# The last four gate pairs of the second block as seven products of half the columns

## The chip, the cores and the metric

One core of a Trainium2 chip runs the whole program in one launch. The metric is the device time of that launch in microseconds. Lower is better. Three runs of the kernel before were timed; one further number is that of the profiled execution.

## The reference, cut to what matters

A first transformer block (differential attention, multiscale pooling, MLP) feeds a second one. The sequence has 512 tokens, the model 1024 features, all in float32. The change is in the second block's mixer and in what follows it directly:

```python
proj = h @ w_in[l]
q_a, k_a, v_a, u_b, gate_b, gate_c, g_a, g_b = jnp.split(proj, split_points, axis=-1)
...
branch_a = o_a @ w_branch_a[l]
branch_b = y_b @ w_branch_b[l]
merged = jax.nn.sigmoid(g_a) * branch_a + jax.nn.sigmoid(g_b) * branch_b
x = x + merged @ w_mix_out[l]
x = x + memory_cross_attention(rms_norm(x, norm_mem_q[l]), rms_norm(mem, norm_mem_kv[l]),
                               w_mem_q[l], w_mem_kv[l], w_mem_o[l])
```

`g_a` and `g_b` have 1024 features each, `branch_a` and `branch_b` come from 512 features, and `mem` has 256 rows of 1024 features.

## The kernel before

Activations lie with features on the 128 partitions and the 512 tokens along the free axis, so a matrix product is made in output tiles of 128 features x 512 tokens. A *unit* is the weights of one such tile: 128 output features, 1024 (or 512) input features, held as 128 x 1024 (or 512) numbers. Every value that goes into a product is split into a rounded high part and a remainder, and each 128 x 128 block of weights takes three products: high with high, high with remainder, remainder with high. A 1024-wide unit has 8 blocks and so 24 products of 512 columns, a 512-wide one 12.

The work is written out by hand as one list of steps (`Order.build`), which every engine walks through in order, taking the steps that concern it. `tick` moves a clock on by one half-unit of products; `later(n, step)` puts a step into the list n ticks after the next one, ahead of that tick's products; `drain` ticks until nothing is left waiting. SyncE issues the loads of weights into `RAW` (three places of 128 x 1024), ScalarE rounds them into `WH` or `WTh` (`split`, `split_hi`), VectorE writes the remainder into `WL` or `WTl` (the same step, `split_lo`), TensorE multiplies. `WH` and `WL` have six halves, numbered 4 to 9; `WTh` and `WTl` have four, 0 to 3. `Places` gives each unit its slot: a wide unit gets the next two of the six, in turn, by the count `wide`:

```python
keys = (4 + 2 * (wide % NW), 5 + 2 * (wide % NW))
wide += 1
...
self.free_after.append(max(self.last_in_slot.get(k, -1) for k in keys))
```

ScalarE waits, before it rounds a unit, until the unit that was last in its slot has been multiplied (`free_after`). Outside the stretches with seven products, a unit is rounded `ahead` = 3 units in advance (`split_to`).

Products of units go to the two banks of `G` in turn; a bank is free again when the step that empties it is done (`g_bank`). In `block_b`, for each n of 0 to 7 there are four units: `sa n` and `sb n` (the two gates, 1024 wide), `bb n` and `ba n` (the two branches, 512 wide). The gate's sum is emptied by ScalarE's sigmoid (`gate_b`) into `sgb`; VectorE multiplies the branch's sum into it (`branch`), and `merge_b` adds the two, rounds on ScalarE, and writes the remainder on VectorE. The merged tile n is chunk n of the products `mx 0` to `mx 7` that follow in `memory`, each with its residual addition on VectorE, a scaled rounded copy and a square on ScalarE. GpSimd sums the squares. Beside gates 2 to 6 the memory tokens are loaded, squared, summed, normed by one product (`norm`, `mem`) and split; `km` needs them after `mx`.

Seven products (Winograd's form of Strassen's scheme) are in the kernel in two other places: 12 pairs of up-projection units in the first block (`seven_up`) and 20 pairs in the last feed-forward layer. A pair of units times 512 tokens is seen as a 2 x 2 matrix of blocks times a 2 x 2 matrix, and computed by seven products of 4 blocks x 3 x 256 columns. It needs sums of weight blocks (`tile_sum`, VectorE), sums of activation blocks (`h`, `s13`, `s2`, `s4`, `s_hi`, `s_lo`) and recombination (`one_out` and `c11` on ScalarE, `w_less`, `v_less`, `c22`, `c12`, `c21` on VectorE).

Of the kernel before, what the change touches and what calls it, by code (L numbers as in the profile page):

```python
# [104 lines left out]
MID, MID_FIRST, MID_PAIRS = 100, 4, 12  # L105
AHEAD_M = 6
RAW_MLP = {("up", 0): (0, 1, 2, 0, 1, 2, 0, 1), ("dn", 0): (2, 0, 1, 2, 0, 2, 0, 1), ("dn", 8): PLACES, ("dn", 16): (0, 3, 0, 0, 2, 1, 0, 2),
# [14 lines left out]
def plan():  # L122
# [23 lines left out]
    for n in range(2, 8):  # L146
        u += [("sa", n, 1024), ("sb", n, 1024), ("bb", n, 512), ("ba", n, 512)]
# [32 lines left out]
class Places:  # L180
# [3 lines left out]
    def __init__(self, units):  # L184
        self.slot, self.free_after, self.third, self.nth, self.loads = [], [], [], [], []
        self.pair_nth, self.last_in_slot, self.last_in_third, self.count = {}, {}, {}, [0] * (NRAW + 1)
        wide, half, cycle, raw = 0, 0, (), 0
        third_of = {(name, i + n): t for (name, i), row in RAW_MLP.items() for n, t in enumerate(row)}
        self.plain_held, self.pair_held = [0] * (NRAW + 1), [0, 0]
        for v, (name, i, width) in enumerate(units):  # L190
            if name == "su":
# [29 lines left out]
    def pairs_over(self, third):  # L221

        return max(self.pair_held) if third == 2 else self.pair_held[third % NRAW]
# [14 lines left out]
class Order:  # L238
# [3 lines left out]
    def __init__(self):  # L242
# [8 lines left out]
        self.fetches, self.pairs = self.tail_loads(), [f for f in range(22) if ("st", f, 0) in self.item_of]  # L251
        self.middle = [MID + p for p in range(MID_FIRST, MID_FIRST + MID_PAIRS)]
# [126 lines left out]
    def split_to(self, u, ahead):  # L379
# [6 lines left out]
        halves = sum(width // S for _, _, width in self.units[u + 1:self.split])  # L386
        while self.split < len(self.units):
# [353 lines left out]

    def attention_b(self, start):
# [11 lines left out]
    def block_b(self):  # L754
# [211 lines left out]
def program(nc, a, out):  # L966
# [4 lines left out]
    first_pairs = (order.middle[0:2], order.pairs[0:2])  # L971
    pairs = order.middle + order.pairs
    unit_at = {u: n for n, u in enumerate((name, i) for name, i, _ in units)}
    ctx = ExitStack()
    with ctx:
# [59 lines left out]
        sgb = [(F[:, 2, :], T[:, 7, :]), (F[:, 0, :], F[:, 1, :])]  # L1035
# [103 lines left out]
        SUMS = T[:, S_AT:S_AT + 2, :].rearrange("p a (b s) -> p (a b) s", b=2)  # L1139

        def halves_of(kt):

            return (F[:, 0, :], F[:, 1, :]) if kt % 2 == 0 else (F[:, 2, :], MSK[:, :])
# [8 lines left out]
        def raw_tile(third):  # L1152

            return RAW[:, third, :] if third < NRAW else T[:, 4:6, :].rearrange("p a s -> p (a s)")

        def b_tiles(f):

            return {"t1": T[:, 4 + 2 * (f % 2), :], "t3": T[:, 5 + 2 * (f % 2), :], "b11": RAW[:, f % 2, 0:S],
                    "b21": RAW[:, f % 2, S:2 * S], "b22": RAW[:, 2, f % 2 * S:f % 2 * S + S], "t2": T_SUM[0], "t4": T_SUM[1]}

# [135 lines left out]
        LOADED, LOADED_BEFORE = (*d_raw, d_x[6]), (0, 0, 0, 2)  # L1296
# [6 lines left out]
        SEVEN_ACT, SEVEN_DVE = tally("one_out", "c11", "silu"), tally("w_less", "v_less", "c22", "c12", "c21")  # L1303
# [22 lines left out]
        def pair_source(f):  # L1326

            return (a["up"][2 * (f - MID)], a["up"][2 * (f - MID) + 1]) if f >= MID else (a["fg"][f], a["fu"][f])
# [25 lines left out]
        def _(e):  # L1354
            cst = a["cst"]
            for step in steps:
# [5 lines left out]
                elif kind == "load" and places.loads[arg[0]][0] != "unit":  # L1362
# [5 lines left out]
                    elif name == "sums" and f == MID + MID_FIRST + 1:  # L1368
                        e.wait_ge(prep_dve, PREP_DVE["s_lo", 0, 3])
                    if behind:  # L1370
# [8 lines left out]
                elif kind == "load" and arg[0] > 0:  # L1379
# [8 lines left out]
                    if behind:  # L1388
                        e.wait_ge(w_hi, behind)
                        e.wait_ge(w_lo, behind)  # L1390
                    e.dma_start(raw_tile(third)[:, 0:c], src).then_inc(LOADED[third], 16)
# [2058 lines left out]
```

## Time and profile before

| what | us |
|---|---|
| median of three runs | 1547.46 |
| lowest and highest | 1547.44, 1548.38 |
| profiled execution, its time | 1548.38 |
| profiled execution, its span (first to last instruction) | 1546.6 |
| TensorE busy | 1536.8 |
| VectorE busy | 1055.0 |
| ScalarE busy | 754.5 |
| GpSimd busy | 69.1 |

The span is what the views of the profile divide up; what the time has beyond it lies outside the instructions. A product's record overlaps the next one's, so its cost is read from the distance of two starts, not from its duration. The gates of n = 2 start at 888.08 us, the mix product at 986.48 us.

### The profile page before, as it was taken

The numbers are of one execution on the slowest core, as the hardware profiler recorded it, in microseconds if no ns is written. First come the engines' busy times: TensorE is split into PE (matmuls) and PEld (weight loads), VectorE is DVE, ScalarE is ACT, GpSimd is POOL, SyncE is SP. The second block draws the span as 40 slices with busy tenths as digits, with TensorE's granted clock in tenths as the row PEclk, the third lists the DMA queues.
The fourth block names the chain that finished last, engine by engine and source line by source line (L and its number), as shares of the span: only waits on it lengthen the run. The fifth ranks groups of instructions, "written<-read, shape, count | busy, mean of one in ns | idle before, by whom it ended". The sixth has DMA issues, their size and how long they took to land.

```text
span 1546.6 us, 22323 instructions
## 1 busy us (share of the span) xinstructions
PE 1536.8 (99%) x8348; PEld 1330.0 (86%) x8348; DVE 1055.0 (68%) x1755; ACT 754.5 (49%) x1307; POOL 69.1 (4%) x60
## 2 busy tenths in 40 slices
PE   9999999999999999999999999999999999999998
PEld 7888888888899899888888888888888899989987
DVE  6776887768789575447777545555555899948735
ACT  5446677744457445444544334344444445524514
POOL 0000000020000000210000010020002000000002
PEclk9999999999999999999999999999999999999999
DMA  5333222332323233324351242334123333322322
GB/s 195 122 109 97 88 78 93 103 129 90 127 84 110 96 96 108 97 82 131 118 141 62 71 137 87 118 118 156 55 82 109 110 103 110 124 96 82 110 89 75
DMA packets 56235, 161.88 MB, mean 105 GB/s; under 512 B 7232, under 2 KB 8640, under 8 KB 56000
## 3 DMA queue, kind: packets, MB, share of 16 engines
q1 hardware_dynamic: 55504, 159.41, 31.7%
q8 instruction: 67, 1.10, 0.3%
q0 software_dynamic: 320, 0.52, 0.2%
q10 hardware_dynamic: 304, 0.52, 0.1%
q14 instruction: 40, 0.33, 0.1%
HBM read 148.89 MB, written 2.10 MB: 98 GB/s over the span
## 4 chain that ended last, share of the span: by engine, by line
PE 96%; DVE 2%; ACT 1%; issue 1%; DMA 1%; SPq 0%; DVEq 0%; ACTq 0%
PE G L1490 66%; PE TP L1490 10%; PE SC L1490 9%; PE O L1490 5%; PE M L1490 5%; PE TP L1946 1%; PE TP L1892 0%; DMA T<-QK 0%; DVE WL L2623 0%; DMA GN<-in_gains 0%; PE TP L1995 0%; ACT L2030 0%; SPq L1465 0%; ACT WH L2033 0%; DVE T L2917 0%
## 5 line engine op out<-in xcount | busy, mean ns | idle before, releaser
L1490 PE MATMUL G<-XGh,WH 128*128 128x512 f32 x920 | 362.2, 394 | 0.0
L2623 DVE TENSOR_TENSOR WL<-RAW,WH 128x1024 fp32r<-128x1024 f32 (+2 forms) x269 | 282.7, 1055 | 116.5 <-ACT WH L2033 116.2
L1490 PE MATMUL G<-XGh,WL 128*128 128x512 f32 x920 | 358.4, 390 | 0.0
L1490 PE MATMUL G<-XGl,WH 128*128 128x512 f32 x920 | 358.3, 389 | 0.0
L2033 ACT ACTIVATE WH<-RAW 128x1024 fp32r<-128x1024 f32 (+2 forms) x275 | 240.0, 881 | 93.3 <-PE G L1490 60.8
L1490 PEld LDWEIGHTS G<-XGh,WL 128*128 128x128 f32 x920 | 172.7, 188 | 36.5
L1490 PEld LDWEIGHTS G<-XGh,WH 128*128 128x128 f32 x920 | 172.8, 188 | 36.1
L1490 PEld LDWEIGHTS G<-XGl,WH 128*128 128x128 f32 x920 | 172.9, 188 | 34.3 <-DVE XGl L2623 0.2
L1490 PE MATMUL G<-MGh,WH 128*128 128x512 f32 x372 | 145.0, 390 | 0.0
L1490 PE MATMUL G<-MGl,WH 128*128 128x512 f32 x372 | 144.8, 389 | 0.0
L1490 PE MATMUL G<-MGh,WL 128*128 128x512 f32 x372 | 144.7, 389 | 0.0
L2973 DVE TENSOR_TENSOR X<-X,G 128x512 f32<-128x512 f32 x67 | 46.0, 686 | 132.8 <-PE G L1490 132.7
L1490 PEld LDWEIGHTS G<-MGh,WL 128*128 128x128 f32 x372 | 69.9, 188 | 14.6
L1490 PEld LDWEIGHTS G<-MGh,WH 128*128 128x128 f32 x372 | 69.8, 188 | 14.5
L1490 PEld LDWEIGHTS G<-MGl,WH 128*128 128x128 f32 x372 | 69.8, 188 | 14.5 <-DVE MGl L2623 0.2
L2590 POOL TENSOR_TENSOR F<-F 128x512 f32<-128x512 f32 x26 | 34.9, 1342 | 698.7 <-ACT F L2132 698.7
L2033 ACT ACTIVATE MGh<-T 128x512 fp32r<-128x512 f32 x38 | 23.9, 629 | 56.0 <-DVE T L3127 20.9
L2033 ACT ACTIVATE XGh<-X,GN 128x512 fp32r<-128x512 f32 x24 | 17.4, 723 | 63.9 <-DVE X L2973 63.9
L1490 PE MATMUL TP<-QK,WH 128*128 128x256 f32 x248 | 46.0, 283 | 0.0
L2033 ACT ACTIVATE QK<-G 128x512 fp32r<-128x512 f32 (+1 forms) x32 | 17.4, 544 | 53.4 <-PE G L1490 51.0
L2033 ACT ACTIVATE WTh<-RAW 128x512 fp32r<-128x512 f32 (+1 forms) x60 | 35.6, 612 | 13.8 <-DMA RAW<-in_f 13.2
L2033 ACT ACTIVATE WH<-T 128x512 fp32r<-128x512 f32 (+1 forms) x38 | 24.6, 648 | 33.8 <-DVE T L3219 29.3
(443 smaller groups left out, 3268.8 us busy)
## 6 DMA issues: line engine op xcount, KB each, us to landing
RAW<-in_dn SPq DMA_DIRECT2D x30, 512.0 KB, 3.3
RAW<-in_fg SPq DMA_DIRECT2D x22, 512.0 KB, 4.2
RAW<-in_up SPq DMA_DIRECT2D x20, 512.0 KB, 3.4
RAW<-in_g SPq DMA_DIRECT2D x16, 512.0 KB, 3.4
RAW<-in_f SPq DMA_DIRECT2D x14, 512.0 KB, 3.7
X<-in_x SPq DMA_DIRECT2D x16, 256.0 KB, 4.3
RAW<-in_q SPq DMA_DIRECT2D x8, 512.0 KB, 3.3
RAW<-in_k SPq DMA_DIRECT2D x8, 512.0 KB, 3.4
```

The costliest lines, as they stand in the source:

```text
L1490: return e.matmul(dst, st, mv, start=start, stop=stop, skip_group_check=True)
L1946: t = e.transpose(TP[:, c, block], weight_pair(3 * p + g, block)[:, c, :], ID[:, :])
L2033: return e.activation(dst, src, ACT.Copy, scale=scale)
L2590: e.tensor_tensor(acc, acc, sqs[arg[1] % 2], ALU.add).then_inc(acc_done, 1)
L2623: return e.tensor_tensor(dst, src, hi.bitcast(F32), ALU.subtract)
L2973: e.tensor_tensor(X[:, n, :], X[:, n, :], bank, ALU.add).then_inc(g_empty, 1)
```

## The change

The gate pairs of n = 4 to 7 are computed by seven products. Their list entry is `sevens(...)` in place of `("sa", n, 1024), ("sb", n, 1024)`. The block sums of the normed input are made in twelve ticks beside n = 0 to 3. Product j of a late pair always has half j (0 to 6), `bb n` half 7 and `ba n` half 8; `bb` and `ba` are loaded into single tiles of `T`. The recombined gates are written to `RB` and `MSK`, which hold n = 3 to 7 in turn, and two or three sigmoids follow. The branch multiplication of n = 4 to 7 is put one product later. `merge_b` becomes `merge_sum` and `merge_b`, both delayed (five and six ticks for n of 3 and more). The memory tokens are loaded in n = 7, and their squares, norm and splits, now three steps (`mem_mul`, `mem_split`, `mem_lo`), are put beside the mix products.

```diff
@@ plan
     for n in range(2, 8):
-        u += [("sa", n, 1024), ("sb", n, 1024), ("bb", n, 512), ("ba", n, 512)]
+        if n < GATE_FIRST:
+            u += [("sa", n, 1024), ("sb", n, 1024)]
+        else:
+            u += sevens(GATED - MID + n, GATED - MID + n + 1)
+        u += [("bb", n, 512), ("ba", n, 512)]
@@ Places
-            if name == "su":
+            if name == "su" and i[0] >= GATED - MID:
+                keys = (i[1],)
+            elif name in ("bb", "ba") and i >= GATE_FIRST:
+                keys = (7 if name == "bb" else 8,)
+            elif name == "su":
                 if units[v - 1][0] != "su":
@@ split_to
+            if v > u and self.units[v][0] == "su" and self.units[v][1][0] == GATED - MID + GATE_FIRST:
+                made += 1
+                if made > 2 and self.units[u][0] != "ba":
+                    break
@@
+    def prepare_gates(self, start):
+
+        for kt in range(4):
+            for n, kinds in enumerate((("h",), ("s13", "s2", "s4"), ("s_hi",), ("s_lo",))):
+                for kind in kinds:
+                    self.later(start + 3 * kt + n, kind, 2, kt)
+
+    def seven_gates(self, i):
+
+        f = GATED + i
+        for j in range(7):
+            self.tick()
+            if j == 0:
+                for n, kind in ((3, "one_out"), (3, "w_less"), (3, "v_less"), (4, "c22"), (5, "c11"), (6, "c12"), (6, "c21")):
+                    self.later(n, kind, f)
+                self.later(6, "sigmoid", f, 1)
+                self.later(7, "sigmoid", f, 0)
+            self.put("seventh", f, j, self.take("su", (f - MID, j)))
@@ block_b
         def branch(n, w):
             self.gemm(("ba", "bb")[w], n, ("branch", n, w))
-            self.put("branch", n, w)
+            if n < GATE_FIRST:
+                self.put("branch", n, w)
+            else:
+                self.later(1, "branch", n, w)
+
+        def merge(n):
+            at = 1 if n < GATE_FIRST - 1 else 4
+            self.later(at, "merge_sum", n)
+            self.later(at + 1, "merge_b", n)
...
+        self.prepare_gates(0)
         for n in range(2):
             branch(n, 0)
-            self.put("merge_b", n)
-        self.put("mem_load")
-        for k in range(8):
-            self.later(4 + k, "sq", "mem", k)
-            self.later(20 + k, "mem_split", k)
-        self.later(17, "norm", "mem")
+            merge(n)
         for n in range(2, 8):
-            gates(n)
+            if n < GATE_FIRST:
+                gates(n)
+            else:
+                self.seven_gates(n)
+            if n == 7:
+                self.put("mem_load")
             branch(n, 1)
             branch(n, 0)
-            self.put("merge_b", n)
+            merge(n)
         self.drain()
 
     def memory(self):
+        for k in range(8):
+            self.later(k // 3, "sq", "mem", k)
+            self.later(5 + k, "mem_mul", k)
+            self.later(6 + k, "mem_split", k)
+            self.later(7 + k, "mem_lo", k)
+        self.later(3, "norm", "mem")
@@ SyncE
                 elif kind == "mem_load":
-                    e.wait_ge(tb_done, TB["turn_b", 3, 2])
+                    e.wait_ge(w_hi, unit("ba", 7))
+                    e.wait_ge(w_lo, unit("ba", 7))
                     e.dma_start(T[:, 0:4, :], a["mem"]).then_inc(d_mem, 16)
@@ VectorE
                 elif kind == "branch":
                     n, w = arg
-                    dst = sgb[n % 2][w]
+                    dst = sgb[n][w]
                     e.wait_ge(unit_done, gemm_done(step))
-                    e.wait_ge(g_moved, MOVED["gate_b", n, w])
+                    if n < GATE_FIRST:
+                        e.wait_ge(g_moved, MOVED["gate_b", n, w])
+                    else:
+                        e.wait_ge(seven_act, SEVEN_ACT["sigmoid", GATED + n, w])
                     e.tensor_tensor(dst, dst, G[:, turn_of[step] % 2, :], ALU.mult).then_inc(g_empty, 1)
```

## Rows read from the trace of the kernel before

**Rows 1.** The page: busy time of the engines; TensorE's granted clock by slices.

```profile
PE 1536.8 (99%) x8348; PEld 1330.0 (86%) x8348; DVE 1055.0 (68%) x1755; ACT 754.5 (49%) x1307; POOL 69.1 (4%) x60
...
PEclk9999999999999999999999999999999999999999
```

**Rows 2.** The page: the chain that ended last, by engine.

```profile
PE 96%; DVE 2%; ACT 1%; issue 1%; DMA 1%; SPq 0%; DVEq 0%; ACTq 0%
```

**Rows 3.** Windows: n = 2, 3 and 7, then five up-projection pairs.

```profile
core 0: us, PE busy (x) PEld busy (x) DVE busy (x) ACT busy (x) POOL busy (x), PEclk, DMA share, GB/s
...
888.08:904.40 16.32, 16.32 (x73) 13.51 (x72) 7.90 (x10) 6.18 (x10) 1.48 (x1) 1.00 0.45 162
904.40:920.72 16.32, 16.32 (x73) 13.51 (x72) 6.64 (x8) 6.83 (x13) 5.90 (x6) 1.00 0.31 98
...
970.16:986.48 16.32, 16.32 (x73) 13.51 (x72) 6.42 (x8) 4.88 (x7) 0.00 (x0) 1.00 0.37 119
...
456.70:507.10 50.40, 50.40 (x422) 50.40 (x421) 48.05 (x89) 37.88 (x76) 0.00 (x0) 1.00 0.32 105
```

**Rows 4.** Timeline of TensorE: start, duration; three places.

```profile
456.70 0.40 PE L1490 MATMUL O<-QK,WH 128*128 128x256 f32 x2
...
934.32 0.59 PE L1807 MATMUL M<-T,ONE 128*128 128x256 f32 x2
...
983.76 0.39 PE L1490 MATMUL G<-MGh,WH 128*128 128x512 f32 x1
...
986.48 0.62 PE L1490 MATMUL G<-QK,WH 128*128 128x512 f32 x2
```

**Rows 5.** Timeline of VectorE, end of the gates and first residual.

```profile
985.11 1.23 DVE L2623 TENSOR_TENSOR WL<-RAW,WH 128x1024 fp32r<-128x1024 f32 x1 [0.47 <-ACT WH L2033]
986.68 0.69 DVE L3092 TENSOR_TENSOR F<-F,G 128x512 f32<-128x512 f32 x1 [0.34 <-PE G L1490]
987.40 0.69 DVE L3098 TENSOR_TENSOR F<-F 128x512 f32<-128x512 f32 x1
```

**Rows 6.** Timeline of ScalarE and VectorE in an up-projection pair.

```profile
461.28 0.39 ACT L2033 ACTIVATE F<-SC 128x256 f32<-128x256 f32 x1
...
461.76 0.42 DVE L3296 TENSOR_TENSOR F<-TP,F 128x256 f32<-128x256 f32 x1
```

**Rows 7.** Timeline of ScalarE, end of the gates.

```profile
984.02 1.06 ACT L2033 ACTIVATE WH<-RAW 128x1024 fp32r<-128x1024 f32 x1 [1.23 <-PE G L1490]
...
988.13 0.63 ACT L2033 ACTIVATE Vh<-F 128x512 fp32r<-128x512 f32 x1 [3.05 <-DVE F L3098]
```

**Rows 8.** The memory tokens: SyncE's issue, ScalarE's first square.

```profile
890.37 0.42 SPq L1480 DMA_DIRECT2D T<-in_mem  x1
...
895.94 0.42 ACT L2132 ACTIVATE T<-T 128x256 f32<-128x256 f32 x1 [1.04 <-DMA T<-in_mem]
```

**Rows 9.** Timeline: the first mix residual and what follows; a memory split.

```profile
961.10 0.48 DVE L3110 SCALAR_TENSOR_TENSOR T<-T,GN 128x256 f32<-128x256 f32 x1
...
992.19 0.69 DVE L2973 TENSOR_TENSOR X<-X,G 128x512 f32<-128x512 f32 x1 [1.22 <-PE G L1490]
...
992.91 0.72 ACT L2033 ACTIVATE XGh<-X,GN 128x512 fp32r<-128x512 f32 x1 [3.20 <-DVE X L2973]
993.54 0.62 ACT L2132 ACTIVATE F<-X 128x512 f32<-128x512 f32 x1
...
993.67 0.75 DVE L2624 SCALAR_TENSOR_TENSOR XGl<-X,GN,XGh 128x512 fp32r<-128x512 f32 x1 [0.79 <-ACT XGh L2033]
...
994.06 1.04 ACT L2033 ACTIVATE WH<-RAW 128x1024 fp32r<-128x1024 f32 x1
```

**Rows 10.** GpSimd's additions of squares; VectorE beside one; shortest, median, longest in ns.

```profile
901.09 1.48 POOL L2590 TENSOR_TENSOR T<-T 128x256 f32<-128x256 f32 x1 [219.65 <-ACT T L2132]
...
900.74 1.23 DVE L2623 TENSOR_TENSOR WL<-RAW,WH 128x1024 fp32r<-128x1024 f32 x1 [5.12 <-ACT WH L2033]
...
L2590 POOL TENSOR_TENSOR T<-T x13: 738/1298/1479, 625.7 to 917.4; 128x256 f32<-128x256 f32 x7, 128x512 f32<-128x512 f32 x6
```

More of the change, by code:

```diff
@@ L251, in __init__ @@
         self.fetches, self.pairs = self.tail_loads(), [f for f in range(22) if ("st", f, 0) in self.item_of]
+        self.gated = [GATED + n for n in range(GATE_FIRST, 8)]
         self.middle = [MID + p for p in range(MID_FIRST, MID_FIRST + MID_PAIRS)]
@@ L970, in program @@
     items, item_of, fetches, places = order.items, order.item_of, order.fetches, order.places
-    first_pairs = (order.middle[0:2], order.pairs[0:2])
-    pairs = order.middle + order.pairs
+    first_pairs = (order.middle[0:2], order.pairs[0:2], order.gated[0:2])
+    pairs = order.middle + order.gated + order.pairs
+    last_gated = order.gated[-1]
     unit_at = {u: n for n, u in enumerate((name, i) for name, i, _ in units)}
@@ L1369, in _ @@
                         e.wait_ge(prep_dve, PREP_DVE["s_lo", 0, 3])
+                    elif name == "sums" and f == GATED + GATE_FIRST:
+                        e.wait_ge(tb_done, TB["turn_b", 3, 2])
+                    elif name == "sums" and f == GATED + GATE_FIRST + 1:
+                        e.wait_ge(mb_lo, MB["merge_b", 2])
                     if behind:
@@ L1618, in _, with left_of_gates @@
             left_of[6] = lambda kt: (Vh[:, 4 + kt, HALF_S:S], Vl[:, 4 + kt, HALF_S:S])
+            def left_of_gates(j, kt):
+                if j in (0, 1, 3, 5):
+                    s = (0, 1, 3, 5).index(j)
+                    h, l = GATE_SUMS[2 * (s // 2):2 * (s // 2) + 2]
+                    return h[:, s % 2, kt, :], l[:, s % 2, kt, :]
+                k, half = kt if j == 2 else 4 + kt, slice(HALF_S, S) if j == 6 else slice(0, HALF_S)
+                return XGh[:, k, half], XGl[:, k, half]
             for step in steps:
@@ L1677, in _ @@
                     mid = f >= MID
-                    first, second = (f == pair for pair in first_pairs[0 if mid else 1])
+                    gated = f >= GATED
+                    first, second = (f == pair for pair in first_pairs[2 if gated else 0 if mid else 1])
                     wh, wl = w_tile(q) if mid else item_tile(q)
@@ L1681, in _ @@
                     bank = bank[:, 0:HALF_S]
-                    if j == 0:
+                    if gated and (j == 0 and (first or second)):
+                        e.wait_ge(ob_lo, PVB["pv_b", 3])
+                    elif gated and first and j in (1, 3):
+                        e.wait_ge(wtb_lo, 2 * 16)
+                    elif gated and (j == 2 and (first or second)):
+                        e.wait_ge(sb_win, 12)
+                    elif j == 0:
                         if first and mid:
@@ L1720, in _ @@
                         at = slice(kt * P, (kt + 1) * P)
-                        hi, lo = left_of[j](kt)
-                        if first and j in (0, 2):
+                        hi, lo = left_of_gates(j, kt) if gated else left_of[j](kt)
+                        if gated and first and j == 0:
+                            e.wait_ge(prep_dve, PREP_DVE["s_lo", 2, kt])
+                        elif first and j in (0, 2) and not gated:
                             e.wait_ge(prep_dve, PREP_DVE["s_lo" if j == 0 else "a_lo", 0 if mid else 1, kt])
@@ L2114, in _ @@
                         e.wait_ge(d_mem, 16)
+                        if k == 0:
+                            e.wait_ge(w_lo, unit("su", (last_gated - MID, 6)))
                     else:
@@ L2526, in _ @@
                     e.wait_ge(*seven_done(f, 4))
-                    e.activation(T[:, f % 2, 0:HALF_S], SC[:, TURN7[f] % 2, 0:HALF_S], ACT.Relu if f >= MID else ACT.Silu).then_inc(
-                        seven_act, 1)
+                    e.activation(made_in(f)[0][:, 0:HALF_S], SC[:, TURN7[f] % 2, 0:HALF_S],
+                                 ACT.Sigmoid if f >= GATED else ACT.Relu if f >= MID else ACT.Silu).then_inc(seven_act, 1)
+                elif kind == "sigmoid":
+                    f, w = arg
+                    table(ACT.Sigmoid)
+                    e.wait_ge(seven_dve, SEVEN_DVE["c12" if w else "c21", f])
+                    part = made_in(f)[1] if w else made_in(f)[0][:, HALF_S:S]
+                    e.activation(part, part, ACT.Sigmoid).then_inc(seven_act, 1)
                 elif kind == "silu":
@@ L3202, in _ @@
                     b, n = b_tiles(f), TURN7[f]
-                    first = f in (first_pairs[0][0], first_pairs[1][0])
-                    section = 0 if f >= MID else 1
+                    first = f in [pair[0] for pair in first_pairs]
+                    section = 2 if f >= GATED else 0 if f >= MID else 1
                     if not first and i in (1, 3):
@@ L3208, in _ @@
                         e.wait_ge(*lo_made)
+                    elif i == 1 and section == 2:
+                        e.wait_ge(mb_lo, MB["merge_b", 1])
                     elif i == 1:
@@ L3237, in _ @@
                     section, kt = arg
+                    if section == 2:
+                        if kt == 0:
+                            e.wait_ge(tb_done, TB["turn_b", 3, 2])
+                        else:
+                            e.wait_ge(prep_dve, PREP_DVE["s4", 2, kt - 1])
+                        for at, k in zip(halves_of(section, kt), (kt, 4 + kt)):
+                            t = e.tensor_tensor(at, XGh[:, k, :].bitcast(F32), XGl[:, k, :].bitcast(F32), ALU.add)
+                        t.then_inc(prep_dve, 1)
+                        continue
                     if kt == 0:
@@ L3241, in _ @@
                         e.wait_ge(prep_dve, PREP_DVE["a_lo", section, kt - 2])
-                    for at, k in zip(halves_of(kt), (kt, 4 + kt)):
+                    for at, k in zip(halves_of(section, kt), (kt, 4 + kt)):
                         t = e.scalar_tensor_tensor(at, X[:, k, :], gain((G_MLP, G_FFN)[section], k), RB[:, :], ALU.mult, ALU.mult)
```

123 lines of the change are left out of this document (89 added, 34 removed).

## The prediction

> **What bounds the kernel now.** I read the page's busy line first: TensorE is busy for 1536.8 of 1546.6 us, and its granted clock stands at the full level in all forty slices [rows 1]. The chain that ended last says the same in another way: 96% of it is TensorE work [rows 2]. So a microsecond of TensorE work removed, or a microsecond in which TensorE has to wait, should move the end by about one microsecond. Everything else is off that path as long as it keeps ahead.
>
> Then I read the stretch that the change touches. The windows give each gate number a stretch of 16.32 us (three of them are shown), TensorE busy for all of it, with 72 weight loads, VectorE busy only 6.4 to 7.9 us and ScalarE 4.9 to 6.8 us [rows 3]. There is no TensorE idle to win back here, only columns.
>
> **The change part by part.**
>
> *Fewer columns.* In the old form a gate pair is two units of 24 products of 512 columns, 48 in all. A gate number's 72 products take 16.32 us, so one takes 0.2267 us and a pair 10.88 us. What seven products cost is in the profile already: in the first block's up projection five pairs fill 50.40 us with 84 products of 256 columns each [rows 3, 4] (421 loads, one more than 5 x 84, at the edge), so a pair takes 10.08 us and a product 0.120 us. The change makes four pairs so: 4 x (10.88 - 10.08) = 3.2 us less. The halving of columns does not halve the time, and this is all there is to gain: 3.2 us of 1547 is 0.21%. (About 0.2%, 3.1 us, is what a measurement of this kernel can tell from no change.)
>
> *More work on VectorE and ScalarE.* A late pair now needs on VectorE 4 tile sums, 7 + 2 weight remainders, 2 branch products, a merge sum and a merge remainder (17 operations at 0.60 us when they follow each other, by the 0.69 us of [rows 5] less the overlap), and 5 of 256 columns at 0.42 us [rows 6]: 10.2 + 2.1 = 12.3 us, some 13.8 us with each at its full length, in a stretch of 10.08 + 5.44 = 15.52 us. The up projection's pairs run with VectorE busy 48.05 of 50.40 us and TensorE loses nothing [rows 3]. I therefore cost the steady pairs at 0. The cover is the lead of up to seven halves (over 10 us of products) at which weights are made; without it each pair would pay about the microsecond by which VectorE is late.
>
> *The first of the four pairs.* The block sums (4 k-tiles, each 2 + 2 operations of 512 and 4 of 256 columns, about 4.1 us of VectorE, 16 us in all) run during gate numbers 2 and 3. VectorE was busy 7.90 + 6.64 of 32.64 us there [rows 3], so they fit, but it arrives at pair 4 with four operations (a tile sum, three remainders, 4 x 0.60 = 2.4 us) that a steady pair has behind it. In the up projection the first recombination copy is over 0.8 us before the fifth product (461.28 + 0.39 against 456.70 + 4 x 1.44 = 462.46) [rows 4, 6]. 2.4 us late less such slack and what VectorE waits for anyway leaves 0.4 to 1 us; I take 0.5, bounds 0 and 2.4.
>
> *The slot of the first mix product.* This decides the case. `Places` gives the two halves of WH and WL out in turn to wide units (`wide` counts on), but the late `bb` and `ba` are given fixed halves 7 and 8 and do not advance `wide`, nor do the new products. Counting the list of units through, `ba 3` has slot 6, so the next wide unit, `mx 0`, gets slot 8 and 9: the first of these is the home of `ba 7`, the unit that TensorE works on directly before `mx 0`. In the kernel before, `mx 0` follows `sb 7` there, with two units between. So `mx 0`'s weights can be rounded only once `ba 7`'s last product has ended. Call T0 the moment at which `mx 0` could start. By the row of the same event for `mx 1` before, whose slot `bb 7` frees when TensorE goes over to the next unit at 983.76, ScalarE starts the 1024-wide copy at 984.02 and ends 1.06 us later; VectorE's remainder starts at 985.11 and takes 1.23 us [rows 5, 7]. That gives T0 + 0.26 to 1.32, and T0 + 1.35 to 2.58. It is worse than that, because both engines work in program order. The list has `mx 0`'s split before `bb 7`'s products and `mx 1`'s before `ba 7`'s, and the branch products of number 7, which are now put one product later, stand behind both on VectorE. `mx 0` writes the G bank that the branch product of `bb 7` has to empty. ScalarE: the last sigmoid (256 wide, 0.42 us as the square in [rows 8]), then `mx 1`'s copy, to T0 + 2.59. VectorE: `mx 1`'s remainder T0 + 2.63 to 3.86, the branch product from T0 + 3.77 to 4.46 (back to back operations overlap by 0.09). TensorE starts at T0 + 4.5. Before, the branch product of `bb 7` came ahead of both. Bounds: 2.6 if only the weights counted, 4.8 with slower handovers; I take 4.5. What is late next: `merge 7` follows at T0 + 5.1, its remainder ends at about 7.2 (the sum of 0.69 us and the copy of 0.63 in [rows 5, 7], a remainder like the sum), and `mx 0` wants it as its eighth chunk at T0 + 4.5 + 4.8 = 9.3. Hidden.
>
> *The memory tiles.* Their load now waits for `ba 7`'s weights, which are made some 13 us before T0; it took 895.94 - 890.37 = 5.6 us to land [rows 8]. Hidden, and it stands in SyncE's queue with mix loads behind it that are needed later. But the squares and their sum, which before had from 895.94 to 934.32 us to be ready in [rows 4, 8], are now put into the first four half-units of the mix product. TensorE's norm product for them stands ahead of the second half of `mx 1`, at 2.72 us after `mx 0` ends (call that D). It needs the last of seven GpSimd additions. The last two squares stand on ScalarE behind `mx 0`'s residual: residual D + 0.27, rounded copy D + 0.99, square of x D + 1.62 [rows 9] less 986.48 + 24 x 0.2267 = 991.92, so the sixth and seventh mem squares start at D + 2.14 and 2.46. An addition of 256 columns took 0.74 us at the shortest, and 1.48 us where VectorE ran a remainder of two inputs beside it [rows 10]. Two, from D + 2.63: to D + 4.2 or 5.6. TensorE waits from D + 2.72: 1.5 to 2.9 us, 4.9 if the earlier additions are all long too and hold up ScalarE. I take 1.9. The norm product itself (0.59 us for its pair [rows 4]) is only moved. The products of `mem_mul`, `mem_split` and `mem_lo` come one of each for each half-unit of 2.72 us, with 0.48 us [rows 9] and, by the 256-column row of [rows 6], 0.42 us of VectorE, and are over a half-unit before the key product; costed at 0. Their cover is the 5.44 us of a mix unit, with 0.69 + 0.75 + 1.23 us of VectorE work in it [rows 5, 9] and 1.8 us more now.
>
> A rule of the Trainium skill bears on the additions: the page SBUF — State Buffer, section SBUF: two separate sides, says that GpSimd and a VectorE operation with two memory inputs take one shared port pair exclusively, so that one of the two stands still. By it an addition beside VectorE would take about double: the row of 1.48 us agrees, and with it the wait would be nearer 2.9 than 1.5 us.
>
> *What goes.* Two activation-table loads and the memory work leave ScalarE in gates 4 to 6; nobody on the path waited for them. Worth 0.
>
> **Sum.** -3.2 + 0.5 + 4.5 + 1.9 = +3.7 us. The profiled execution has a span of 1546.6 us in a time of 1548.38 us, which is 0.9 us above the median of the three runs, 1547.46. I add the sum to the median: 1551.2 us.
>
> **Rivals.**
>
> *B, the norm wait is hidden.* If the additions keep up, only 4.5 - 3.2 + 0 to 0.5 remain: 1548.8 to 1549.3, no change that can be told. For it: the shortest addition of [rows 10] is half the longest. Against: the last squares are behind `mx 0`'s residual in program order whatever their length.
>
> *C, the other side: the refill costs nothing.* If `mx 0`'s weights did not have to wait for `ba 7`, the branch products would not stand behind them, and the sum is -3.2 + 0.5 + 1.9 = -0.8 us, 1546.7; with the norm hidden as well 1544.3 to 1544.8. It decides where the wait at `mx 0` is under 3.2 - 0.5 - 1.9 = 0.8 us: from there the kernel is no slower. For it: no wait of this kind is in the profile before. Against: the slots as counted.
>
> *D, as forecast, and the clock.* The granted clock is full in every slice before, but TensorE was also idle for only 9.8 us in all [rows 1]. If it falls to the 1.2 GHz level after that gap, products take 0.453 instead of 0.2267 us: half a unit to one unit of the mix product at that level costs 2.7 to 5.4 us more; 3.5 gives 1554.7. The Trainium skill has a rule for this (TensorE: Matmul & The Clock Gate, section HAM oscillation — how this bites in real kernels): a long enough gap between bursts of products sends the clock back to its low level. No row here shows a gap that long.
>
> *E, VectorE paces the new pairs.* 13.8 of 15.52 us is more than double its share of before, with waits for ScalarE between; if each pair ends up 1 us late it is +4 on top, 1555. Against: the 48.05 of 50.40 us.
>
> **How the numbers follow.** Forecast (both waits) 0.50, own range 1549.8 to 1556, of which 0.42 lies above 1550.6; B 0.16; C 0.14; D 0.10; E 0.10. Slower by over 0.2%: 0.42 + 0.10 + 0.09 = 0.61. Faster by over 0.2% needs all of the 3.2 us and no wait: 0.04. The rest, 0.35, is within 0.2%. The range leaves out the lowest of C and the highest of the forecast, D and E: 1546.0 to 1556.5.
>
> **What the profile after would show.** Right: pairs 4 to 7 at 10.08 us each; an idle of about 4.5 us of TensorE before `mx 0`, ended by VectorE's branch product, with the 1024-wide copy starting 0.26 us after `ba 7`; a second idle of 1.5 to 3 us before the norm product, ended by GpSimd. Wrong: no idle before `mx 0` (then I miscounted the slots), additions finished before the norm product is due, idles inside the four pairs (then VectorE is the bound there), or a granted clock under 1.00 after the gap.

## The result and the profile after

| what | before | after |
|---|---|---|
| median, us | 1547.92 (4 runs, 1547.44 to 1548.38) | 1557.23 (4 runs, 1556.24 to 1559.74) |
| profiled execution, its time | 1548.38 | 1559.74 |
| its span | 1546.6 | 1557.9 |

The ratio is 1.0060, 95% interval 1.0048 to 1.0072: the kernel is 0.6% slower, 9.3 us in the medians. The forecast was 1551.2 us with a range up to 1556.5. The direction was right, and the loss came out 5.6 us larger than forecast (9.3 against 3.7). The profiled execution is the slowest of the four; a part of its 11.4 us over the execution of before is not the change's. The first load of `sa` was issued 1.47 us later (818.45 against 816.98 us), and of this 1.43 us were already there at the first load of the up projection (328.40 against 326.97 us), far upstream of the change. In the twelve profiled executions of this document that load goes out between 326.24 and 328.42 us, and both ends belong to kernels with the change.

First the page: the busy line and the granted clock (for [rows 1]).

```profile
PE 1539.1 (99%) x8492; PEld 1338.6 (86%) x8492; DVE 1098.0 (70%) x1843; ACT 766.9 (49%) x1341; POOL 67.6 (4%) x60
...
PEclk9999999999999999999999999999999999999999
```

TensorE's busy time rose although it has fewer columns to do, and VectorE has 43 us more. The clock line shows nothing: a slice is 39 us long, and a dip of 4 us in it is rounded away. So the next view is TensorE's waits: what it waited for, whose work ended the wait, microseconds in total, times, longest.

```profile
PE G L1565 <- DVE MSK L3215: 4.3, 1, 4.3
PE SC L1565 <- ACT F L2127: 2.1, 2, 1.9
PE M L1901 <- POOL T L2710: 1.5, 1, 1.5
PE SC L1710 <- DVE ONE L2776: 1.1, 1, 1.1
PE TP L1986 <- DVE WTl L2743: 0.8, 1, 0.8
...
PE G L1565 <- DVE QK L2743: 0.5, 1, 0.5
```

The list of the kernel before begins with the same 1.1 us and has nothing else over 0.4 us. The first three are the change's: in front of `mx 0`, inside the pair of n = 4, and in front of the memory tokens' norm product. So is the last, of 0.5 us, just behind the mix product. The 0.8 us for `WTl` stand at 173 us and belong to the upstream part. The timeline of TensorE at the three places (start, duration, in brackets the idle before it and its releaser), for [rows 4]:

```profile
927.83 0.28 PE L1565 MATMUL TP<-Vh,WTl 128*128 128x256 f32 x1
930.06 0.39 PE L1565 MATMUL SC<-XGh,WH 128*128 128x256 f32 x1 [1.95 <-ACT F L2127]
...
931.35 0.28 PE L1565 MATMUL SC<-XGl,WH 128*128 128x256 f32 x1
931.47 0.30 PE L1565 MATMUL SC<-XGh,WL 128*128 128x256 f32 x1
...
932.42 0.42 PE L1565 MATMUL O<-Vl,WH 128*128 128x256 f32 x1
932.63 0.42 PE L1565 MATMUL O<-Vh,WL 128*128 128x256 f32 x1
...
987.82 0.39 PE L1565 MATMUL G<-MGh,WL 128*128 128x512 f32 x1
992.52 0.80 PE L1565 MATMUL G<-QK,WH 128*128 128x512 f32 x2 [4.31 <-DVE MSK L3215]
993.12 0.63 PE L1565 MATMUL G<-QK,WL 128*128 128x512 f32 x1
...
1004.08 0.67 PE L1901 MATMUL M<-T,ONE 128*128 128x256 f32 x2 [1.48 <-POOL T L2710]
```

`mx 0` could have started 0.22 us after 987.82, at 988.04, and started at 992.52: 4.48 us. Two products are 0.12 us apart at 931.35 and 0.21 us apart at 932.42: the clock has fallen. The windows show it: the start of the four pairs, one steady pair with its two branches, and three stretches around `mx 0` (for [rows 3]; the granted clock is the number ahead of the DMA share).

```profile
921.00:936.50 15.50, 13.55 (x93) 13.03 (x93) 12.26 (x23) 7.61 (x15) 0.00 (x0) 0.89 0.59 193
936.12:951.66 15.54, 15.54 (x109) 14.58 (x109) 12.60 (x22) 6.96 (x13) 0.00 (x0) 1.00 0.30 102
...
986.50:992.50 6.00, 1.70 (x8) 1.08 (x6) 3.08 (x4) 2.31 (x3) 0.00 (x0) 1.00 0.14 32
992.50:996.50 4.00, 3.98 (x10) 3.13 (x11) 2.10 (x4) 2.68 (x6) 1.22 (x2) 0.57 0.59 214
996.50:1000.00 3.50, 3.50 (x17) 2.86 (x16) 1.34 (x2) 0.96 (x3) 3.07 (x4) 1.00 0.32 85
```

A steady number takes 15.54 us with TensorE busy throughout, as forecast. After the gap in front of `mx 0` the granted clock is 0.57 in a stretch of 4 us, most of it at the 1.2 GHz level. The unit took until 999.72, 7.20 us instead of 24 x 0.2267 = 5.44: 1.76 us more. In the fifth number (n = 4) the wait of 1.95 us is followed by low-clock products from 931.6 to 935.0 us, some 16 of them at 0.21 instead of 0.12 us: 1.4 us more.

Who was late for `mx 0`? ScalarE, then VectorE (for [rows 5, 7]):

```profile
988.30 1.06 ACT L2127 ACTIVATE WH<-RAW 128x1024 fp32r<-128x1024 f32 x1 [5.88 <-PE G L1565]
...
989.57 1.04 ACT L2127 ACTIVATE WH<-RAW 128x1024 fp32r<-128x1024 f32 x1
```

```profile
989.39 2.48 DVE L2743 TENSOR_TENSOR WL<-RAW,WH 128x1024 fp32r<-128x1024 f32 x2 [6.12 <-ACT WH L2127]
991.78 0.68 DVE L3215 TENSOR_TENSOR MSK<-MSK,G 128x512 f32<-128x512 f32 x1
```

The copy starts 0.26 us after `ba 7` ends; the two remainders follow it, and the branch product that empties the G bank comes last. And who was late in the pair of n = 4? The recombination copy `F<-SC` (929.64 us) stood on ScalarE behind two tiles of n = 5, and those came from sums on VectorE that waited for a load:

```profile
927.42 0.69 DVE L3354 TENSOR_TENSOR T<-RAW,T 128x512 f32<-128x512 f32 x1 [1.55 <-DMA RAW<-in_sa]
```

That load was issued late, because it stood in SyncE's queue behind the one of `bb 4`, which waits for the last block sum (VectorE, ended at 919.27). That wait is new with the change:

```diff
+                    elif name in ("bb", "ba") and i == GATE_FIRST:
+                        e.wait_ge(prep_dve, PREP_DVE["s_lo", 2, 3])
```

SyncE's timeline:

```profile
919.29 0.33 SPq L1465 DMA_DIRECT2D T<-in_bb  x1
919.97 0.33 SPq L1465 DMA_DIRECT2D T<-in_ba  x1
920.41 0.36 SPq L1444 DMA_DIRECT2D T<-in_sb  x1
920.87 0.38 SPq L1446 DMA_DIRECT2D RAW<-in_sb  x1
921.34 0.38 SPq L1448 DMA_DIRECT2D RAW<-in_sa  x1
```

### The profile page after: what moved, and what is told of

It reads as the page before. It is cut to its first block and busy times, and to the rows that moved or that the text cites. A ratio compares the mean times of both kernels' runs of the same rounds, so it can differ in the third digit from the quotient of the medians.

```text
span 1557.9 us, 22821 instructions
## 1 busy us (share of the span) xinstructions
PE 1539.1 (99%) x8492; PEld 1338.6 (86%) x8492; DVE 1098.0 (70%) x1843; ACT 766.9 (49%) x1341; POOL 67.6 (4%) x60
## 5 line engine op out<-in xcount | busy, mean ns | idle before, releaser
L1565 PE MATMUL G<-XGh,WH 128*128 128x512 f32 x856 | 337.8, 395 | 0.0
L1565 PE MATMUL G<-XGh,WL 128*128 128x512 f32 x856 | 333.9, 390 | 0.0
L1565 PE MATMUL G<-XGl,WH 128*128 128x512 f32 x856 | 333.8, 390 | 0.0
L2743 DVE TENSOR_TENSOR WL<-RAW,WH 128x1024 fp32r<-128x1024 f32 (+2 forms) x260 | 271.0, 1048 | 83.2 <-ACT WH L2127 83.1
L2127 ACT ACTIVATE WH<-RAW 128x1024 fp32r<-128x1024 f32 (+2 forms) x266 | 231.0, 877 | 97.0 <-PE G L1565 65.9
L1565 PEld LDWEIGHTS G<-XGh,WL 128*128 128x128 f32 x856 | 160.8, 188 | 34.0
L1565 PEld LDWEIGHTS G<-XGh,WH 128*128 128x128 f32 x856 | 160.9, 188 | 33.4
L1565 PEld LDWEIGHTS G<-XGl,WH 128*128 128x128 f32 x856 | 161.0, 188 | 31.7 <-DVE XGl L2743 0.2
L2127 ACT ACTIVATE WTh<-RAW 128x512 fp32r<-128x512 f32 x64 | 38.1, 613 | 14.6 <-DMA RAW<-in_f 13.8
L2127 ACT ACTIVATE WTh<-T 128x512 fp32r<-128x512 f32 (+1 forms) x40 | 23.4, 586 | 41.0 <-DVE T L3354 30.5
```

The costliest lines, as they stand in the source:

```text
L1565: return e.matmul(dst, st, mv, start=start, stop=stop, skip_group_check=True)
L2127: return e.activation(dst, src, ACT.Copy, scale=scale)
L2743: return e.tensor_tensor(dst, src, hi.bitcast(F32), ALU.subtract)
```

## The experiments

Ten kernels, all of them computing the whole function. Each is compared with the kernel before on the same chip; that kernel's median was 1548.7 to 1548.9 us there, 0.8 to 1.0 us above its median beside the changed kernel. So losses against it, not times, are compared with the 9.3 us of the change. The interval of that loss is 7.4 to 11.1 us; the other kernels' losses have intervals of about 1.4 us to either side with 11 runs and 1.9 us with 5.

### Each wait mended alone, and all three

*The slot*, in `Places`: the count is moved on by one at `mx 0`, so that it takes a slot whose last unit is long multiplied.

```diff
             elif ...:
+                if (name, i) == ("mx", 0):
+                    wide += 1
                 keys = (4 + 2 * (wide % NW), 5 + 2 * (wide % NW))
```

> The changed kernel with one more step of the slot count ahead of the first mix product, so that it takes halves 4 and 5 (last used by the sixth product of pair 7) and not half 8, which the branch unit directly before it holds. Theory (the slot): the TensorE wait of about 4.5 us before the first mix product shrinks to 0.5 us (what is left is the branch product behind the second mix unit's remainder), and the low clock after it, worth 1.8 us, goes with it: 5.7 us less than the changed kernel, about 1551.5 us against 1557.2. Rival (VectorE or the delayed branch product is the cause, the slot only lies beside it): the wait stays over 3 us and the time within 2 us of the changed kernel.

Measured: 1551.2 us (1549.4 to 1553.1, 11 runs), ratio 1.0016, interval 1.0007 to 1.0025. The wait at `mx 0` is 0.3 us (TensorE's waits of this kernel), and the granted clock is 1.00 in every window from 880 to 1060 us:

```profile
PE M L1903 <- POOL T L2712: 1.5, 1, 1.5
...
PE SC L1567 <- ACT F L2129: 1.0, 1, 1.0
...
PE G L1567 <- DVE MSK L3217: 0.3, 1, 0.3
```

This single count is worth about 6.8 us of the 9.3 (9.3 lost by the change, 2.5 left). The two profiles show 5.6 of them at `mx 0`: 4.0 us less wait and 1.6 us less for its 24 products. The other 1.2 us are within the intervals.

*The order of the loads*: those of `bb 4` and `ba 4` are issued after those of the seven products of n = 5.

```diff
                 if i[1] == 0:
+                    late = self.loads[-2:]
+                    if i[0] == GATED - MID + GATE_FIRST + 1:
+                        del self.loads[-2:]
                     self.seven_loads(v, i[0])
+                    if i[0] == GATED - MID + GATE_FIRST + 1:
+                        self.loads += late
```

> The changed kernel with the three loads of gate pair 5 issued ahead of the loads of branch units bb 4 and ba 4, which wait for the block sums. Theory (late weights): pair 5's loads then go out at about 915 instead of 921 us, VectorE no longer stands 1.5 us on them, the first recombination copy is in time, the 1.95 us wait of TensorE inside pair 4 and the low clock after it (1.4 us) and most of the 0.5 us VectorE wait go: 3.3 us less, about 1553.9 us. Rival (VectorE is too full in front of pair 4, as the prediction had it): the loads come early, but the wait stays at 1 us or more and the time drops by under 1.5 us.

Measured: 1556.2 us (1555.1 to 1556.9, 5 runs), ratio 1.0047, interval 1.0034 to 1.0059. The 1.95 us fell to 0.3 (the line has a second wait, of 0.2 us), and the stretch from 920 to 940 us has a clock of 1.00, where the changed kernel's was 0.83 from 930 on:

```profile
PE SC L1570 <- ACT F L2132: 0.5, 2, 0.3
```

The mechanism holds, the amount does not: 3.3 us less were expected, and the medians show about 1.8, with intervals that overlap. The profiled execution of the changed kernel was the slowest, and in the profiles of three other kernels without this edit the wait was 1.0, 1.35 and 1.4 us with no low clock after it. So by the traces the edit takes away 0.7 to 1.1 us where the clock stays up, and 3.0 us in the execution where it fell.

*The norm of the memory tokens*, one half-unit later.

```diff
-        self.later(3, "norm", "mem")
+        self.later(4, "norm", "mem")
```

> The changed kernel with the memory norm one half-unit later, ahead of the third mix unit and not inside the second. Theory (the GpSimd additions are 1.5 us late for their product): the wait ended by GpSimd is gone and nothing takes its place, 1.5 us less, about 1555.7 us. Rival (the splits of the memory tokens then come late for the key product): a wait of VectorE or ScalarE before the first key product, time unchanged.

Measured: 1557.2 us (1556.2 to 1557.9, 5 runs), ratio 1.0054, interval 1.0041 to 1.0066. The wait for GpSimd is gone from the list. In the medians this is worth 0.8 us, half of the 1.5 expected and within the intervals. The trace shows why it is not more: at the first key product, just behind the mix stage, TensorE now waits 1.3 us in two waits, where the changed kernel had 0.5. The rival was half right.

```profile
PE G L1565 <- DVE QK L2743: 1.0, 1, 1.0
...
PE G L1565 <- DVE X L3093: 0.3, 1, 0.3
```

In this profiled execution the clock had fallen before the first product of `mx 0` at 989.73 (its mean is 0.93 from 985.00 to there and 0.50 behind) and stayed low until 995.9 us, for 6.2 us of products. The unit's 24 products took until 998.19, so 8.46 us instead of 5.44:

```profile
989.73 1.22 PE L1565 MATMUL G<-QK,WH 128*128 128x512 f32 x2 [4.31 <-DVE MSK L3215]
...
995.44 0.60 PE L1565 MATMUL G<-Vl,WH 128*128 128x512 f32 x1
```

*All three.*

> The three edits together: slot, loads, norm. If the three waits and the two low-clock stretches are all that the change added, 3.2 us of columns are gained against the kernel before, less 0.5 us before the first mix product: 1545.2 us against 1547.9. If some of the 9.3 us lies elsewhere (the profile of the changed kernel is already 1.4 us late before the changed stretch and loses 1 us after it), about 1547.5 us. Rival (the clock falls for another reason than the waits, or VectorE paces the pairs): over 1549 us, with the granted clock still under full in the stretch.

Measured: 1549.4 us (1548.2 to 1550.7, 11 runs), ratio 1.0004, interval 0.9995 to 1.0013. Of 9.3 us, 8.6 are gone. But it does not beat the kernel before, and I had expected it to: the 3.2 us of columns are not in the time. The time is where the rival had it, but not for the rival's reason, since the granted clock is 1.00 in every window from 880 to 1060 us. Its list of waits says where to look:

```profile
PE G L1572 <- DVE QK L2750: 1.0, 1, 1.0
...
PE G L1572 <- DVE X L3100: 0.3, 1, 0.3
```

The two waits stand at 1035.88 and 1031.76 us, just behind the mix product, where TensorE waited for nothing before. VectorE there, between two residual additions (`X<-X,G`):

```profile
1014.44 0.68 DVE L3100 TENSOR_TENSOR X<-X,G 128x512 f32<-128x512 f32 x1
1015.92 0.75 DVE L2751 SCALAR_TENSOR_TENSOR XGl<-X,GN,XGh 128x512 fp32r<-128x512 f32 x1 [0.79 <-ACT XGh L2134]
1016.59 1.52 DVE L2750 TENSOR_TENSOR WTl<-T,WTh 128x256 fp32r<-128x256 f32 x1
...
1018.61 1.22 DVE L2750 TENSOR_TENSOR WL<-RAW,WH 128x1024 fp32r<-128x1024 f32 x1
1019.74 0.42 DVE L2750 TENSOR_TENSOR WTl<-T,WTh 128x256 fp32r<-128x256 f32 x1
...
1020.67 0.68 DVE L3100 TENSOR_TENSOR X<-X,G 128x512 f32<-128x512 f32 x1
```

The round is 20.67 - 14.44 = 6.23 us, and TensorE's unit is 5.44. The same remainder of a memory tile takes 0.42 us in one place and 1.52 in the other. GpSimd's timeline has the reason, an addition of squares that runs exactly there:

```profile
1016.48 1.34 POOL L2717 TENSOR_TENSOR F<-F 128x512 f32<-128x512 f32 x1 [4.88 <-ACT F L2239]
```

The remainder ends 0.29 us after that addition. In the kernel before, VectorE waited for ScalarE at this moment, and its next operation, of 1024 columns, was held for 0.3 us only (1.52 us against 1.22):

```profile
1016.90 1.52 DVE L2623 TENSOR_TENSOR WL<-RAW,WH 128x1024 fp32r<-128x1024 f32 x1 [0.72 <-ACT WH L2033]
```

This is the port that GpSimd and VectorE share, as the Trainium skill has it (SBUF — State Buffer, section SBUF: two separate sides): of a VectorE operation with two inputs in SBUF and a GpSimd operation that reads SBUF, the one that starts first keeps the port for its whole length, and the other stands still. The trace agrees: the addition started first, and the remainder took 1.52 instead of 0.42 us.

### The shared port in the mix stage

The three edits, and the additions of the squares of `mx 3` to `mx 7` on VectorE.

```diff
-ADDS = (("mlp", 7), ("c1", 7), ("c2", 7), *(("attn", k) for k in range(1, 8)))
+ADDS = (("mlp", 7), ("c1", 7), ("c2", 7), *(("mq", k) for k in range(3, 8)), *(("attn", k) for k in range(1, 8)))
...
             self.put("sq", "mq", n)
+            if n >= 3:
+                self.put("add", "mq", n)
```

> The three edits, and the additions of the squares of mx 3 to mx 7 on VectorE (about 0.69 us each) instead of GpSimd (1.34 us each). Theory: the gain of the seven products is lost at the end of the mix stage because each memory tile's remainder that VectorE makes beside GpSimd's addition takes 1.52 us instead of 0.42 us, so that its round is 6.22 us where TensorE's unit is 5.44 us; without GpSimd's additions the small remainders take 0.42 us, the round is 5.1 to 5.5 us, TensorE's waits of 0.27 and 0.99 us behind mx 7 go, and the time is 1548.1 us (1547.8 to 1548.6). Rival (VectorE is simply full with the memory tiles there; an addition more only fills it further): the round stays at 6 us or more, the waits stay or grow, 1549.4 us or above.

Measured: 1547.9 us (1546.7 to 1549.0, 11 runs), ratio 0.9994, interval 0.9985 to 1.0002. Both waits behind `mx 7` are gone. VectorE's round:

```profile
1015.84 0.75 DVE L2753 SCALAR_TENSOR_TENSOR XGl<-X,GN,XGh 128x512 fp32r<-128x512 f32 x1 [0.79 <-ACT XGh L2136]
1016.50 0.68 DVE L2792 TENSOR_TENSOR F<-F 128x512 f32<-128x512 f32 x1
1017.11 0.42 DVE L2752 TENSOR_TENSOR WTl<-T,WTh 128x256 fp32r<-128x256 f32 x1
...
1021.57 0.75 DVE L2753 SCALAR_TENSOR_TENSOR XGl<-X,GN,XGh 128x512 fp32r<-128x512 f32 x1 [0.79 <-ACT XGh L2136]
```

One more operation on VectorE makes its round shorter: 21.57 - 15.84 = 5.73 us instead of 6.23. The theory had 5.1 to 5.5; at 5.73 the lag, 0.3 us a round, is small enough to disappear. That it disappears in the 0.97 us for which VectorE stood idle ahead of each residual addition in the kernel before is my reading, not shown by a run. The rival, that VectorE is simply full, is out.

### The wait at mx 0, taken apart

*The slot alone, in the kernel before.* The count is moved on by two, so that `mx 0` takes `ba 7`'s slot; the gates are plain and the branch is put at once.

```diff
+                if (name, i) == ("mx", 0):
+                    wide += 2
```

> The kernel before with one edit: mx 0 takes the weight slot that the last down projection leaves, as the change makes it do; the gates stay plain and the gated branch is still put at once. It prices the slot alone. Theory (the slot is the cause of most of the 4.48 us in front of mx 0): TensorE now waits 2.6 to 3.2 us there (ScalarE's copy 1.06 us and VectorE's remainder 1.2 us can only start once the slot is free at about 986.5 us, and the remainder stands behind the branch and the sum, 0.69 us each), where the kernel before waits for nothing; if the clock stays at 2.4 GHz the time is about 1551.7 us against 1548.7 us, and if it falls as it did after the 4.48 us gap about 1553.4 us. Rival (the moved branch is the cause): no wait over 0.5 us at mx 0 and the time of the kernel before, 1548.7 us.

Measured: 1554.2 us (1551.6 to 1555.1, 5 runs), ratio 1.0036, interval 1.0022 to 1.0050. TensorE's timeline in the profiled execution, which took 1551.64 us:

```profile
989.63 0.72 PE L1492 MATMUL G<-QK,WH 128*128 128x512 f32 x2 [3.06 <-DVE F L3094]
```

So the slot alone costs 3.1 us of wait. (The bracket counts from the modelled end of the last product; by the distance of the starts, in which the changed kernel had 4.48, it is 3.22 us.) The clock stayed at 1.00 behind it here. The other four executions took 2.3 to 3.5 us more than this one; they were not profiled, so a low clock in them is a guess.

*The branch put at once, in the changed kernel.*

```diff
-            if n < GATE_FIRST:
+            if n < GATE_FIRST or (n, w) == (7, 1):
                 self.put("branch", n, w)
```

> The changed kernel with one edit: the last gated branch is put at once, as it was before, and all else stays as changed. Theory: the 4.48 us in front of mx 0 are the weight slot (about 3.1 us, as the run of the slot alone showed) and the branch product, which stands behind two copies and two remainders (about 1.4 us); with the branch at once TensorE waits 3.0 to 3.3 us there. The time is then 1.3 us under that of the changed kernel if the clock falls after the gap as before (1556 us), and 3 us under it if the clock stays (1554 us). Rival (the weights alone set the start of mx 0, the branch is only the last name): the wait stays at 4.3 to 4.5 us and the time at 1557.2 us.

Measured: 1555.3 us (1554.9 to 1556.7, 5 runs), ratio 1.0044, interval 1.0031 to 1.0056. The wait at `mx 0` is 3.06 us where the changed kernel had 4.31, so the late branch made the other 1.25:

```profile
989.43 0.72 PE L1565 MATMUL G<-QK,WH 128*128 128x512 f32 x2 [3.06 <-DVE MSK L3215]
```

The clock fell again, from 990.4 to 993.8 us. The loss is 6.5 us, 2.8 less than the change's, where the wait alone gives 1.25; the intervals overlap, and the pair of n = 4 alone differs by that much between executions (1.42 us at full clock in this profile, 1.95 and the low clock in that of the changed kernel).

*The same in the version with the three edits.*

> The changed kernel with the slot, the order of the loads and the memory norm mended (as in the run of all three), and also the last gated branch put at once instead of one product later. Theory: with the slot free early, the late branch is what still holds mx 0 for 0.35 us, so this wait goes and the time is 1549.0 us (0.2 to 0.5 us under the 1549.4 us of the three edits). Rival (the branch put at once collides with VectorE's tile work at the end of the gates, which is why it would be moved): the wait stays or grows beyond 0.5 us, and the time is 1549.4 to 1550.5 us.

Measured: 1549.2 us (1547.6 to 1550.1, 11 runs), ratio 1.0002, interval 0.9993 to 1.0011. The wait of 0.35 us at `mx 0` is gone and no new one stands in the list; the medians, 0.2 us apart, cannot tell the two kernels apart.

### All edits, and all but the slot

Slot, loads, norm, branch and additions together:

> All five edits together: slot, order of the loads, memory norm, last branch at once, additions of mx 3 to mx 7 on VectorE. Theory: none of the waits that the change brought is left but 0.3 to 0.5 us at the fifth pair, so that what the smaller products save is seen: 1547.3 us (1546.6 to 1548.2) against 1548.7 us of the kernel before. Rival (the saving is taken by something that these waits don't show): 1548.5 us or above, no difference from the kernel before.

Measured: 1547.3 us (1545.9 to 1548.8, 11 runs), ratio 0.9990, interval 0.9982 to 0.9999. That is the change without its waits: 1.6 us better than the kernel before, by the interval 0.2 to 2.8, where the sum gives 3.2 less the 0.5 of small waits in the pair of n = 4, so 2.7; and still within the 0.2% that counts as no change here. The profiles say the same: from the first load of `sa` to the last group of products it is 720.33 us here and 721.87 before, 1.5 us less. Of the 1.1 us that are missing, 0.56 lie behind the mix stage's last norm, spread without a wait over 0.2 us. In TensorE's timeline from `mx 0` (985.34 us) to the first product of the next norm (1043.73) it takes 58.39 us, against 1044.39 - 986.48 = 57.91 before; the 0.48 us are the memory tokens' norm product, which is only moved.

The same without the slot's edit:

> All five edits but the slot: mx 0 takes the home of ba 7 again. It prices the slot in the version in which nothing else waits. Theory: a wait of 3.0 to 3.3 us at mx 0, no other new wait; 1550.4 us if the clock stays at 2.4 GHz after it, 1552 us if it falls. The slot alone in the kernel before cost 5.4 us in the median with a wait of 3.1 us and no low clock in the one execution that was profiled (2.9 us above the kernel before), so this also asks whether a gap of 3.1 us brings the low clock. Rival (the slot costs more than its own wait, by lateness of ScalarE and VectorE in the mix stage): new waits of TensorE of over 0.5 us after mx 0, and 1551 us or more at a full clock.

Measured: 1551.7 us (1550.8 to 1553.6, 11 runs), ratio 1.0018, interval 1.0009 to 1.0027. The windows from the start of `mx 0`:

```profile
987.19:991.00 3.81, 3.81 (x10) 2.99 (x11) 3.07 (x4) 1.37 (x4) 0.05 (x1) 0.55 0.75 227
991.00:995.00 4.00, 4.00 (x19) 3.32 (x18) 1.86 (x2) 2.27 (x5) 3.57 (x4) 1.00 0.20 67
```

A wait of 3.06 us, the same as in the kernel before with the slot, and this time the clock is at 0.55 over the first 3.81 us. The products up to the one at 991.40 took 4.21 us, where the same ones took 992.27 - 989.63 = 2.64 us in the execution with the full clock: 1.57 us more. By the starts, the gap is 3.22 us and the unit takes 7.16 instead of 5.44: 4.9 us, of which the medians show 4.4, the amount by which this kernel is slower than the one above. There is no other new wait: the slot costs its gap and what the clock adds, nothing later.

## Why the prediction was wrong

*The wait in front of `mx 0`: right.* Forecast 4.5 us, measured 4.48, and by the steps given: copy at T0 + 0.26, the two remainders, then the branch product from T0 + 3.74 to 4.42. The parts are 3.22 us for the slot and 1.25 for the branch, each shown by a kernel of its own.

*The clock after it: the first step that failed.* Rival D had the mechanism (the clock falls after that gap) and a chance of 0.10, so its price was left out of the sum. It belonged in: the clock fell in each of the three profiles with the 4.48 us gap and in two of three with the shorter one. D's price, 2.7 to 5.4 us, was too high for two of the three: there the 24 products took 1.76 us (the changed kernel) and 1.71 us more, in the third 3.02. The sentence "no row here shows a gap that long" was true, but it was no argument against D: with a rule that speaks for the fall and no row against it, the likeliest case includes it. By that rule of the Trainium skill (TensorE: Matmul & The Clock Gate, section HAM oscillation — how this bites in real kernels) a long gap is followed by the low level; the 4.48 us gap agrees.

*The first of the four pairs: the second step, and the term that was mis-sized most.* I took 0.5 us, bounds 0 and 2.4, from VectorE's backlog. The wait was 1.95 us and the low clock behind it 1.4 in the profiled execution, and 1.0 to 1.4 us without the low clock in three others. The cause was another than the one I costed: not VectorE's queue but SyncE's. The load of `bb 4` waits for the last block sum, and I never asked what stands behind it there. The loads of n = 5 did; the kernel with the two loads moved shows it. So my sign "idles inside the four pairs (then VectorE is the bound there)" came true with a wrong reading: VectorE itself stood waiting for a load.

*The norm of the memory tokens: right.* Forecast 1.9 us, the trace has 1.48 plus a slow first product, about 1.5; [rows 10] gave the lower end, and GpSimd's last two additions took 1.59 us for both. They started ahead of VectorE's remainder and were not held by it, so the upper bound of 2.9 us that I took from the shared port was not reached. Mending it gained only 0.8 in the medians.

*The memory tiles, costed at 0: wrong.* The cover was said to be the 5.44 us of a mix unit. VectorE's round was 6.2 us, because GpSimd's addition held the small remainder for 1.1 us. In the changed kernel this shows as 0.5 us only, since the norm's wait holds TensorE up inside the same stage; with the norm moved it costs about 1.3 us. [rows 10] held the row for it, and I applied it to GpSimd's side alone.

*The columns and the steady pairs: right.* Pairs of n = 5 to 7 come every 15.54 us (15.52 forecast) with TensorE never idle, so rival E is out. C is out by the wait, B by the norm's 1.5 us.

The sum by the profiled execution: -3.2 + 1.95 + 1.4 + 4.48 + 1.76 + 1.5 + 0.5 = +8.4 us, with 1.47 us that were there before the changed stretch. Between this and the +3.7 us of the forecast lie 2.85 us of the first pair, 1.76 of the clock at `mx 0` and 0.5 of the memory tiles, less 0.4 of the norm. It leaves 1.5 us of the 11.4 open; 0.7 of them lie behind the stage's last norm product and the rest before it, in no wait over 0.2 us. In the medians, 9.3 us, mending three waits gave back 8.6.

## What to carry to other kernels

When a form of work gets its own fixed buffers, count through which buffer the next ordinary user is dealt: here one step of a counter cost 6.8 us, twice what the change could save. For each load that gets a new wait, list the loads behind it in the same queue before costing VectorE. And where the engine that bounds the kernel is given a gap of some microseconds, put the low clock behind it into the sum: here it added 1.7 to 3.0 us to a gap of 4.48.

## What was not expected of the hardware

The low clock does not follow the gap alone. At `mx 0` the products are the same in all profiles, so their time shows it (gap by the distance of the starts; 5.44 us is the unit in the kernel before):

| gap, us | the 24 products, us | low clock |
|---|---|---|
| 0.50 (three profiles) | 5.57 to 5.58 | none |
| 3.22 (slot alone, kernel before) | 5.59 | none |
| 3.22 (all but the slot) | 7.16 | 3.4 us, from 0.2 us behind the restart |
| 3.22 (branch put at once) | 7.20 | 3.4 us, from 0.9 us behind the restart |
| 4.48 (loads moved) | 7.15 | 3.4 us, from the restart on |
| 4.48 (changed kernel) | 7.20 | 3.4 us, from 0.5 us behind the restart |
| 4.48 (norm moved) | 8.46 | 6.2 us of products, fallen before the restart |

The gap of 1.95 us in the pair of n = 4 was followed by the low clock too (products 0.21 instead of 0.12 us, from 1.5 us behind the restart, for 3.4 us), and gaps of 0.98, 1.35, 1.42 and 1.48 us never were in these profiles. What decides between these is open; each row but the first is one execution.

Moving an addition from the idle GpSimd (1.34 us) onto VectorE (0.68 us) made VectorE's own round 0.5 us shorter.
